# The first half's down projection: beside the first half's last experts, or between the attention steps of the last half

## What is computed

```python
x = x + (silu(conv3(h @ w_up_a)) * conv3(h @ w_up_b)) @ w_down   # (512 x 2816) @ (2816 x 1024)
return rms_norm(x, final_g)
```

## Time and profile before

| what | value |
|---|---|
| runs shown | 2977.74, 2984.08, 3005.13 us, median 2984.08 |
| profiled execution, its time | 2992.01 us |
| its span, first to last instruction | 2990.2 us |
| mean granted clock of PE | 0.897 of full speed |
| busy: PE, DVE, ACT, POOL | 2533.2, 1781.5, 1130.7, 706.2 us |
| gathered by the experts | 536.90 MB in 512 gathers |
| `w_down` loads | 44 of 512 KB (22 for each half) |
| last gather issued | 2338.5 us from the start |
| last experts' sum added to X | 2362.5 to 2363.8 us |

### The profile page before, as it was taken

How to read it: one execution, slowest core, us unless ns; L and a number is a source line. 1 busy time by engine, 2 the same in 40 slices (tenths; PEclk the granted TensorE clock), 3 DMA queues, 4 the chain that set the end, 5 groups by cost and what they waited for, 6 DMA issues and landing times.

```text
span 2990.2 us, 29389 instructions
## 1 busy us (share of the span) xinstructions
PE 2533.2 (85%) x10046; PEld 1804.9 (60%) x10046; DVE 1781.5 (60%) x4240; ACT 1130.7 (38%) x2747; POOL 706.2 (24%) x566
## 2 busy tenths in 40 slices
PE   8999998889987759788968886688879399788998
PEld 6786765767763346546636643456754287655883
DVE  2101312689687688667889998778897506412430
ACT  2101312242535653544343685465551314412210
POOL 0000000222244344332223565343233101100100
PEclk9999999899998889999988688899989685699999
DMA  6545243789999999998889998899999640032553
GB/s 200 175 152 165 93 159 107 282 307 369 370 409 417 359 389 418 416 371 302 313 334 403 413 371 342 328 409 417 417 418 418 261 135 11 1 106 85 153 151 119
DMA packets 156646, 827.11 MB, mean 277 GB/s; under 512 B 16920, under 2 KB 20392, under 8 KB 90704
## 3 DMA queue, kind: packets, MB, share of 16 engines
q0 software_dynamic: 73728, 536.90, 44.9%
q1 hardware_dynamic: 78144, 276.21, 26.5%
q10 hardware_dynamic: 4624, 12.11, 1.1%
HBM read 816.74 MB, written 8.41 MB: 276 GB/s over the span
## 4 chain that ended last, share of the span: by engine, by line
PE 56%; DVE 18%; ACT 12%; DMA 9%; issue 4%; POOL 1%; ACTq 0%; DVEq 0%; SPq 0%
PE ps L848 25%; DMA BIG<-in_uv,BIG 7%; PE ps L868 6%; PE ps L869 5%; DVE BIG L1871 5%; DVE X L1851 4%; PE ps L849 3%; PE ps L1085 3%; ACT L1372 2%; PE ps L989 2%; PE ps L1107 2%; PE ps L1108 2%; PE ps L1057 2%; DMA BIG<-head_scratch 1%; PE ps L1036 1%
## 5 line engine op out<-in xcount | busy, mean ns | idle before, releaser
L2088 POOL DMA_INDIRECT BIG<-in_uv,BIG x512 | 663.6, 1296 | 1664.5 <-DVE X L1851 575.4
L848 PE MATMUL ps<-BIG,RING 128*128 128x256 f32 x3472 | 804.1, 384 | 15.9 <-DMA RING<-in_w_cq 4.8
L848 PEld LDWEIGHTS ps<-BIG,RING 128*128 128x128 f32 x3472 | 667.7, 193 | 134.5 <-issue 26.7
L1871 DVE CUSTOM_DVE_ANT_0 BIG<-BIG 128x1024 f32<-128x1024 f32 x512 | 618.9, 1219 | 64.6 <-DMA BIG<-in_uv,BIG 63.1
L1851 DVE SCALAR_TENSOR_TENSOR X<-BIG,small,X 128x1024 f32<-128x1024 f32 x351 | 450.3, 1283 | 103.7 <-ACT small L1376 103.5
L1372 ACT ACTIVATE small<-small 128x1 f32<-128x1 f32 x512 | 102.2, 200 | 632.3 <-DVE small L1871 629.7
L848 PE MATMUL ps<-WK,RING 128*128 128x256 f32 x1232 | 287.3, 385 | 18.7 <-DVE BIG L1630 16.7
L848 PEld LDWEIGHTS ps<-WK,RING 128*128 128x128 f32 x1232 | 235.9, 193 | 58.8 <-DVE BIG L1630 23.9
L868 PE MATMUL ps<-RING,BIG 128*128 128x512 f32 (+1 forms) x448 | 225.1, 584 | 7.3 <-DVE BIG L1609 4.4
L869 PE MATMUL ps<-RING,BIG 128*128 128x512 f32 (+1 forms) x448 | 224.4, 582 | 0.0
L1205 ACT ACTIVATE BIG<-ps 128x256 f32<-128x256 f32 (+2 forms) x143 | 56.4, 397 | 398.0 <-PE ps L849 338.3
(11 more groups left out here) (255 smaller groups left out, 3294.4 us busy)
## 6 DMA issues: line engine op xcount, KB each, us to landing
RING<-in_w_up SPq DMA_DIRECT2D x88, 512.0 KB
RING<-in_w_down SPq DMA_DIRECT2D x44, 512.0 KB
RING<-in_w_pq SPq DMA_DIRECT2D x32, 512.0 KB
RING<-in_w_cc SPq DMA_DIRECT2D x16, 512.0 KB
RING<-in_w_cx SPq DMA_DIRECT2D x16, 512.0 KB
RING<-in_w_cb SPq DMA_DIRECT2D x16, 512.0 KB
RING<-in_w_cv SPq DMA_DIRECT2D x16, 512.0 KB
RING<-in_w_gc SPq DMA_DIRECT2D x16, 512.0 KB
```

Of the source, the lines that this page charges most:

```text
L848: e.matmul(ps[:, 0:256], W[:, j, :], src[:, j, 0:256], start=j == 0, stop=False)
L1871: e.tensor_tensor_reduce(out=u, in0=HF[:, t % 2, :], in1=u, scale=1.0, scalar=0.0, op0=ALU.mult, op1=ALU.add, accum_out=dots[:, k % 8:k % ...
L2088: e.indirect_dma_start(out=slot[i], out_offset=None, in_=I["uv"], in_offset=bass.IndirectOffsetOnAxis(ap=IDX[:, t, c:c + 1], axis=0)).then ...
```

## The change

The down projection of half 0 leaves `second(0)`. `late_down` yields it as 44 pieces, first all 22 chunks for token tile 0, then all 22 again for tile 1, each piece with a load of its chunk and two matmuls. In `second(1)` eight pieces stand before the transposes of mix2, one or two behind each nsa step, seven entries (the last six pieces and the mark) before the transposes of `y`. The last norm and the store of half 0 come behind `ou` of half 1. Each half gets buffers of its own; those of half 1 are in the row slots, which are free by then. The wait for the first half's store goes. An expert of tiles 2 and 3 costs 2.5.

```diff
+    def late_down(self):
+        for i in range(2):
+            for f in range(22):
+                k = self.next_ring()
+                yield (0, "chunk", "down", f, k), (1.7, "down", 0, f, k, (i,))
+        yield (0, "mark", ("out", 0)),
...
     def second(self, h, lean):
+        rest = self.late_down() if h else None
+        def beside(n):
+            for steps in (islice(rest, n) if h else ()):
+                yield from steps
...
-        yield from self.norm(("mix2", h), lean, 3.0)
+        yield from self.norm_steps(("mix2", h), lean)
+        yield from beside(8)
+        for k in range(8):
+            yield (3.0 if k == 7 else 0), "trans", ("mix2", h), k, lean
+        self.norming = False
...
             yield step
+            yield from beside(1 + step[3] % 2)
...
         yield 0, "y_norm", h
+        yield from beside(7)
...
         yield from self.proj_tok("ou", h, 2, lean)
+        if h:
+            yield from self.last(0)
         yield from self.cross(2, h, lean)
...
-        for f in range(22):
-            k = self.next_ring()
-            yield 0, "chunk", "down", f, k
-            yield 3.4, "down", h, f, k
-        yield 0, "mark", ("out", h)
+        if h:
+            for f in range(22):
+                k = self.next_ring()
+                yield 0, "chunk", "down", f, k
+                yield 3.4, "down", h, f, k, (0, 1)
+            yield 0, "mark", ("out", h)
+            yield from self.last(h)
+
+    def last(self, h):
         for kind in ("final_in", "final_sq", "final_inv", "final_root", "final_out"):
             yield 0, kind, "fb", h
         yield 0, "store", h
...
-                yield (3.1 if t < 2 else 2.65), "pace"
+                yield (3.1 if t < 2 else 2.5), "pace"
...
+        L = [L0, SLOT0 + 8448]
+        QN = [at_(o, 4, 256) for o in L]
...
+        AF = [at_(o, 22, 256) for o in L]
...
-                    growing.clear()
+                    growing.difference_update(ps_of[site, h, c, t] for t in range(2))
...
-            def down(h, f, k):
+            def down(h, f, k, tiles):
...
-                for q in range(4):
+                qs = [2 * t + hh for t in tiles for hh in range(2)]
+                for q in qs:
                     t, hh = q // 2, q % 2
+                    if f == 0:
+                        bank("dn", h, q)
+                        growing.add(ps_of["dn", h, q])
+                    ps = banks[ps_of["dn", h, q]]
...
+                    if f == 21:
+                        growing.discard(ps_of["dn", h, q])
...
-                return [("total", 1 if h == 0 else 3), ("idx", 2, 3)] + ([("out", 0, 0), ("out", 0, 1)] if h else []) + [
+                return [("total", 1 if h == 0 else 3), ("idx", 2, 3)] + [
```

More of the change, by code:

```diff
@@ L1 @@
 from contextlib import ExitStack
+from itertools import islice
 import numpy as np
@@ L482, in col, with row @@
             return cols[:, COL_AT[name] + i:COL_AT[name] + i + n]
-        def row(name):
+        def row(name, h=0):
             o = ROW_AT[name]
-            v = LROW if o >= 1024 else LNROW
+            v = LROW if o >= 1024 else LNROW[h]
             return v[:, o % 1024:o % 1024 + dict(ROWS)[name]]
@@ L625, in norm_of @@
             if kind == "mix2":
-                return dict(src=half(h), g="mix2", dst=HTz, tmp=TMPz, o=0, pool=False)
+                return dict(src=half(h), g="mix2", dst=HTz[h], tmp=TMPz, o=0, pool=False)
             if kind == "ffn2":
-                return dict(src=half(h), g="ffn2", dst=HTu, tmp=at_(L0, 2, 1024), o=0, pool=False)
+                return dict(src=half(h), g="ffn2", dst=HTu, tmp=at_(L[h], 2, 1024), o=0, pool=False)
             if kind == "o":
@@ L659, in place @@
             if site == "qn":
[L660 removed]
+                return QN[h][:, m, :], 0.125
             if site == "kn":
@@ L924, in cross @@
                 site = "cq" if layer == 1 else "xq"
-                QT = QT1 if layer == 1 else QT2
+                QT = QT1 if layer == 1 else QT2[h]
                 if i < 8:
@@ L1307, in cross @@
                 site = "cq" if layer == 1 else "xq"
-                OT = HT1 if layer == 1 else HTx
+                OT = HT1 if layer == 1 else HTx[h]
                 u = i - 1
@@ L1388, in final_in @@
                     w.wait_ge(*at[name])
-                load(f"{tag}{h}", FG1[tag], bass.AP(I["final_g1" if tag == "fa" else "final_g"].tensor, 0, [[0, 128], [1, 1024]]),
+                load(f"{tag}{h}", FG1[tag][h], bass.AP(I["final_g1" if tag == "fa" else "final_g"].tensor, 0, [[0, 128], [1, 1024]]),
                      tag, h)
@@ L1404, in nsa_gate @@
                     w.wait_ge(*at["mark", ("s2n", h), q])
-                load(f"ln{h}", LNROW, bass.AP(I["rows"].tensor, 0, [[0, 128], [1, 1024]]), "lnrow", h)
+                load(f"ln{h}", LNROW[h], bass.AP(I["rows"].tensor, 0, [[0, 128], [1, 1024]]), "lnrow", h)
             def cmp_in(h, s, i, k):
@@ L1469, in nsa @@
                     w.wait_ge(*at["mm", "nv", h, u])
-                    e.activation(Y[:, qb % 2, 64 * hd:64 * hd + 64], banks[ps_of["nv", h, u]][:, 0:64], ACT.Copy).then_inc(
+                    e.activation(Y[h][:, qb % 2, 64 * hd:64 * hd + 64], banks[ps_of["nv", h, u]][:, 0:64], ACT.Copy).then_inc(
                         act.sem, act("ev", "nv", h, u))
@@ L1878, in final_out @@
                 o = FINAL_AT[tag]
-                dst, fin = (half(h), "fin1") if tag == "fa" else (OUT, "fin")
+                dst, fin = (half(h), "fin1") if tag == "fa" else (OUT[h], "fin")
                 w.wait_ge(*at["rstd", (tag, h)])
@@ L1882, in final_out @@
                 for i in range(2):
-                    e.scalar_tensor_tensor(out=dst[:, i, :], in0=X[:, 2 * h + i, :], scalar=small[:, o + i:o + i + 1], in1=FG1[tag],
+                    e.scalar_tensor_tensor(out=dst[:, i, :], in0=X[:, 2 * h + i, :], scalar=small[:, o + i:o + i + 1], in1=FG1[tag][h],
                                            op0=ALU.mult, op1=ALU.mult).then_inc(dve.sem, dve(fin, h, i))
@@ L2016, in y_norm, with down @@
                         sig = ("nrm", ("y", h), i) if j == 2 else ("yn", h, i, j)
-                        e.tensor_scalar(Y[:, i, a:b], Y[:, i, a:b], small[:, o:o + 1], None, ALU.mult).then_inc(dve.sem, dve(*sig))
-            def down(h, f, k):
+                        e.tensor_scalar(Y[h][:, i, a:b], Y[h][:, i, a:b], small[:, o:o + 1], None, ALU.mult).then_inc(dve.sem, dve(*sig))
+            def down(h, f, k, tiles):
                 if f == 21:
-                    for q in range(4):
+                    for q in range(2 * tiles[0], 2 * tiles[-1] + 2):
                         w.wait_ge(*at["mm", "dn", h, f, q])
```

92 lines of the change are left out of this document (44 added, 48 removed).

## The result

The change makes the kernel 0.8% faster: 2968.1 us (median of 19 runs) against 2995.4 for the kernel before in the same comparison, a ratio of 0.9918, 95% interval 0.9898 to 0.9939. The forecast was 2959 against a median of 2984.1, so 0.84% faster. The profiled execution spans 2967.5 us, against 2990.2 before: 22.7 us less, where the prediction had a sum of 25. The ratio's agreement hides that two of its terms were off and one explanation was too weak; the experiments are about those.

A forecast was written before the change was run, and what follows sets the result against it. DMA bytes were taken to bound the expert stretch from 1900, PE at clock 0.50 the last attention. Terms -35 + 0.4 + 8 + 0 + 2 = -25 us from 2992.0 gave 2967; the median 8 lower, so 2959, range 2934 to 2990.

The forecast's parts named there:

- Parts 1 and 2: Expert stretch: fewer bytes (31 us) and expert price 2.65 to 2.5 (4 us) bring the total 35 us earlier.
- Rival B: Expert stretch: DVE or the order becomes the limit, so parts 1 and 2 give 10 us, not 35: 2984; chance 0.13.
- Part 3: Before mix2's transposes: eight pieces, 13.7 us, meet 12.43 us of idle PE; cost +0.4 us.
- Part 4: Last half's attention: thirty pieces add 51 us, but mean clock rises to 0.95; with 2 us of stops, +8 us.
- L1085-like: Sign of being right: such rows take 0.43 us each in the last half's attention.
- Part 5: Before the transposes of y: six pieces hidden in 15.25 us of idle PE; cost 0, bounds -2 and +5.
- Part 6: Half 0's last norm and store behind ou of half 1: +2 us, the store +0.
- which lie beside the norm's two squares on ACT: Behind ou: half 0's two DVE norm products (2.48 us) overlap the next norm's squares, some 2.4 us.
- D: Last half's attention: pieces don't lift the clock; a loss below c = 0.80, 3032 us at 0.60; chance 0.08.
- C: Expert stretch's DMA gaps fill too (-45 us) and the attention's clock is 1.00: 2941 us; chance 0.18.

The follow-up runs named there:

- the profiled execution without the loads: Kernel before the change, half 0's 22 down steps reading an old ring buffer instead of loading w_down, all matmuls kept: 2973.9 us, ratio 0.9939; profiled span 2989.9.
- eight useless ones: Kernel before the change plus four unread 128x512 identity matmuls behind each of the last half's first two attention steps: 2953.5 us, ratio 0.9879.
- the spread version: Changed kernel with half 0's last norm and store moved into half 1's down steps and the 44 pieces spread over idle stretches and attention: 2948.7 us, ratio 0.9850.
- the first half version: The spread version with only the second eleven of half 0's 22 down chunks moved, as 22 pieces, three by the attention's first step: 2971.4 us, ratio 0.9935.

## Why the prediction was right, and where it was not

The sum came out within 2 us in part by luck. Against the terms as predicted the stages differ by +4.5 us (the expert stretch), +0.8, -4.5 (the attention), -0.6 and +1.5, and these cancel.

**Parts 1 and 2, the expert stretch: -30.5 for -35, with the two terms mis-sized.** The bytes were counted well: up to the last dot product 767.70 MB were moved before and 755.27 after, 12.4 MB less (predicted 13.1), at 418 GB/s 29.7 us, and the last dot product comes 29.3 earlier. What failed is that the terms were added: 31 for the bytes, and 4 on top for the price. At the old price the same bytes gave only 18.5 us (the last dot product at 2339.67), and the price gave the other 10.8, as DMA moved 4.8 MB more by 2227. The count of five experts was right (4.6 by the bytes); what failed was the 1.5 us charged for each of them in the attention. They cost next to nothing there (10.8 us gained by 4.6 of them), near the bound of 12. Less to load is time gained only where the order has the gathers early enough to use it, and what the prediction took for an extra (five experts into the gaps, 4 us) was part of the first term's condition. Rival B's limit is there in the profiled execution without the loads. In the changed kernel VectorE waits for the gathers; that this is because more of the last experts are summed on PE was not tested by itself.

**Part 3: +1.2 for +0.4.** The pieces did meet the idle time, and took 13.97 us (predicted 13.7). The term left out was their start: they wait until VectorE has added the total, and so begin 1.4 us into the 12.43. They overrun by 3.0 us in place of 1.3, and the upper level gives back 1.8 (16.8 us from the total to the first `qn` before, 17.9 now).

**Part 4, the case's hinge: +3.5 for +8.** The predicted mean clock of 0.95 was measured at 0.94, and PE had no gap. The stops for banks and for finished tiles, 2 us, aren't in the rows. What was left out is the pause of 2.90 us at 2474.65, which lies across the start of the window that the prediction counted from the earlier trace rows: the pieces fill it. These two are about the difference between +8 and +3.5. The rows that the prediction's list calls L1085-like are the down matmuls, 75.37 us for 176 rows, 0.43 each. In the changed kernel they are L1117, and behind the first pieces a piece of four takes 1.91 us and two of them 3.63, so 0.45 to 0.48: the sign came true, nearly. The reason given was too weak: I argued from a mixture in which sums stand between the steps, as if the long matmuls had to keep coming. The runs show that it is enough to have them at the start. Behind the last of eight useless ones, or of eight pieces, or of four pieces, the level held for 74 to 75 us. What loses it is less clear. It was gone after pauses of 1.53 us (the spread version) and 2.71 us (the first half version), each with light work behind, and not after one of 2.76 us with the long pieces right behind (2333.46); and in the 64x16 matmuls ahead of the attention it went without any pause. The two terms of the step were measured apart: thirty pieces cost 51.9 us (predicted 51) behind the attention, and the useless matmuls gain 41 us in the attention even after their own 9.3 us, so 51 in all with the 2.9 of the pause (predicted 52 for the clock). They cancel, as the sum had it, but they are two separate things, and the second could be had without the change.

The rule of the Trainium skill ("TensorE: Matmul & The Clock Gate", section "Loop structure matters more than you think"), that matmuls which wait for transfers between them run cold, was set against the edit. Behind the first ones the pieces ran at 1.8 to 1.9 us, the upper level, since their chunks were there and PE had no gap. The rule's half that a wait lets the clock fall is borne out by the timeline of the first half version, where the 2.71 us were a wait for VectorE; the 2.76 us ahead of the pieces at 2333.46 did not do it. Its good case, matmuls back to back, doesn't suffice by itself: PE was busy 65.00 us of 65 at 0.50. The Trainium skill (the same page, section "Part 4: PE-mode transpose") also says that a transpose doesn't count as a busy TensorE in the same way as a matmul for the clock. No run here has transposes alone, but with products of 64 columns and logits of 64 rows among them the level held for 74 us.

**Part 5: -0.6 for 0.** Within its bounds, -2 and +5.

**Part 6: +3.5 for +2.** The step that failed is "which lie beside the norm's two squares on ACT". They stand ahead of them (2628.81 before 2631.41): the norm's squares wait for a mark in VectorE's order that counts the products too. The kernel with the norm moved on gives 3.1 us of it back at this place.

**The chances.** Much of the range was within reach of how the pieces are placed: behind the attention they cost 41.9 us, a loss as in D; at the front of it, with only half of them moved, the kernel is 2.0% faster, beyond C. D got 0.08 because PE has no holes here; what would have decided it, what PE does in the few microseconds behind the first pieces, was in no row that I read.

## What to carry to other kernels

Where TensorE is full at its lower clock, look for what would raise it before moving work in or out: a few of the longest matmuls at the start of the stretch may be worth more than the whole change, and an idle gap right behind them may lose it all. Place work moved out of a transfer-bound stretch into idle stretches first. That the rest is cheaper where the transfers hide it is likely and not shown: half moved was 2.0% faster than before with the clock up and 0.7% with the clock lost, all of it 0.8 to 1.5%, with the last norm's place and the raise of the clock also differing. And freed bytes become time only if the order (here the planner's price of an expert) brings the other transfers forward.

## What the runs showed of the hardware

The granted clock has a memory that the busy share doesn't show. The same attention, with PE full, ran at 0.50 for 106 us before the change and for 72 us in the first half version, and at 1.00 for 74 us behind eight 128x512 matmuls that computed nothing. Both levels hold under the same work; in these runs what stood ahead of it, and the pauses near its start, went with which one it was.

What moves the level is shown only in part. It went to 0.50 in the 64x16 matmuls ahead of the attention with PE busy 4.00 of 4 us, and in every kernel here the attention, or the pieces right ahead of it, begin at that level. It fell behind pauses of 1.53 and 2.71 us, and held through pauses of 0.93, 0.94 and 2.76 us, the last with long matmuls behind it. And it came up by itself late in the attention, at 2580 in the kernel before, at 2552 with thirty pieces behind, and at 2549 in the first half version. No run here isolates why.

The level may also be what spreads the executions of one kernel. In the three later comparisons the kernel before was executed 79 times: 45 executions took up to 2992.3 us, with a mean granted clock of 0.893 to 0.902, the other 34 up to 3017.9, with 0.885 to 0.895. Only one execution of it was traced, so in which stretch they differ is not known.
